# Last steps of the recurrent layer: u split ahead of the scan, another order of loads, two merge tiles ahead of the last gate products

## What is computed

```python
def rglru_block(x, w_in, conv_w, conv_b, w_a, b_a, w_i, b_i, lam, w_out):
    proj = jnp.einsum("bsd,de->bse", x, w_in)
    u, gate = jnp.split(proj, 2, axis=-1)
    u_pad = jnp.pad(u, ((0, 0), (CONV_WIDTH - 1, 0), (0, 0)))
    u = conv_b + sum(u_pad[:, tap:tap + S] * conv_w[tap] for tap in range(CONV_WIDTH))
    ub = u.reshape(B, S, RNN_BLOCKS, RNN_BLOCK_WIDTH)
    r = jax.nn.sigmoid(jnp.einsum("bsnc,ncd->bsnd", ub, w_a).reshape(B, S, RNN_WIDTH) + b_a)
    i = jax.nn.sigmoid(jnp.einsum("bsnc,ncd->bsnd", ub, w_i).reshape(B, S, RNN_WIDTH) + b_i)
    log_a = -LRU_C * r.astype(jnp.float32) * jax.nn.softplus(-lam.astype(jnp.float32))
    a = jnp.exp(log_a)
    bterm = jnp.sqrt(-jnp.expm1(2.0 * log_a)) * (i * u).astype(jnp.float32)
    _, h = lax.associative_scan(combine, (a, bterm), axis=1)   # h[t] = a[t] h[t-1] + bterm[t]
    y = h.astype(x.dtype) * jax.nn.silu(gate)
    return jnp.einsum("bse,ed->bsd", y, w_out)
```

## Time and profile before

| | |
|---|---|
| time, median of 3 runs | 2415.93 us (2414.43 to 2416.19) |
| span of the profiled execution | 2414.6 us |
| PE busy | 2365.7 us, 98% |
| VectorE, ScalarE, GpSimd busy | 1354.1, 1121.3, 617.7 us |
| granted PE clock, 2150 to 2200, 2200 to 2250, 2250 to 2300 us | 1.00, 0.97, 0.97 |
| PE busy in the same three stretches of 50 us | 45.6, 47.5, 46.1 us |

### The profile page before, as it was taken

The page is one execution under the profiler, slowest core; times in us unless marked ns, Lnnn a source line. Parts: engine busy times, 40 slices in busy tenths (PEclk is TensorE's granted clock), DMA queues, the critical chain, the costliest instruction groups (busy, mean ns, idle before and its releaser), DMA issues. The chain is left out here.

```text
span 2414.6 us, 36438 instructions
## 1 busy us (share of the span) xinstructions
PE 2365.7 (98%) x13373; PEld 2031.6 (84%) x13373; DVE 1354.1 (56%) x2772; ACT 1121.3 (46%) x2060; POOL 617.7 (26%) x718
## 2 busy tenths in 40 slices
PE   9999999999999999999999999999999999999998
PEld 7888889998888888888888888878888888887787
DVE  4221211331106888888888888836535565767733
ACT  2111111311116888888888888812014565657300
POOL 0000000000001555545555545516420000000343
PEclk9999999999999999999999999999999999999999
DMA  6443443332234455555445665275533354538762
GB/s 211 139 121 112 116 128 108 118 124 83 84 110 103 110 117 125 136 137 117 112 112 124 137 136 117 78 246 183 187 106 119 119 159 131 148 124 256 243 232 78
DMA packets 221258, 328.77 MB, mean 136 GB/s; under 512 B 17421, under 2 KB 144717, under 8 KB 215261
## 3 DMA queue, kind: packets, MB, share of 16 engines
q1 hardware_dynamic: 220568, 325.91, 47.7%
q0 software_dynamic: 512, 0.53, 0.1%
HBM read 199.89 MB, written 126.48 MB: 135 GB/s over the span
## 5 line engine op out<-in xcount | busy, mean ns | idle before, releaser
L985 DVE TENSOR_TENSOR at_pl<-at_tps,at_ph 128x512 fp32r<-128x512 f32 (+3 forms) x640 | 371.0, 604 | 15.9 <-ACT at_ph L908 15.9
L908 ACT ACTIVATE at_ph<-at_tps 128x512 fp32r<-128x512 f32 (+3 forms) x640 | 318.6, 537 | 125.4 <-PE at_tps L822 117.4
L822 PE MATMUL at_tps<-ident,at_probs 128*128 128x128 f32 x2176 | 340.4, 274 | 8.4 <-DVE at_pl L985 7.1
L380 ACT ACTIVATE pa_stg<-pa_ps 128x512 fp32r<-128x512 f32 (+1 forms) x120 | 71.7, 598 | 575.4 <-PE pa_ps L272 569.5
L842 PE MATMUL at_ops<-at_ph,at_val 128*128 128x256 f32 (+1 forms) x1152 | 315.4, 296 | 0.2 <-DVE at_pl L985 0.2
L898 ACT ACTIVATE at_probs<-at_probs,at_least 128x128 f32<-128x128 f32 (+15 forms) x256 | 308.1, 1204 | 0.0
L272 PE MATMUL pa_ps<-pa_xh,pa_wh 128*128 128x512 f32 x760 | 298.9, 393 | 0.0
L272 PE MATMUL pa_ps<-pa_xh,pa_wl 128*128 128x512 f32 x760 | 297.3, 391 | 0.0
L272 PE MATMUL pa_ps<-pa_xl,pa_wh 128*128 128x512 f32 x760 | 296.9, 391 | 0.0
L842 PE MATMUL at_ops<-at_pl,at_val 128*128 128x256 f32 (+1 forms) x1152 | 295.0, 282 | 0.0
L808 PE MATMUL at_sps<-at_k,at_q 128*128 128x512 f32 (+3 forms) x640 | 277.7, 434 | 9.7 <-DVE at_probs L977 7.2
(11 more groups left out here) (203 smaller groups left out, 4516.0 us busy)
## 6 DMA issues: line engine op xcount, KB each, us to landing
at_q<-q_halves SPq DMA_DIRECT2D x45, 512.0 KB
at_k<-k_halves SPq DMA_DIRECT2D x45, 512.0 KB
q_halves<-pa_stg SPq DMA_DIRECT2D x32, 512.0 KB, 3.8
k_halves<-pa_stg SPq DMA_DIRECT2D x32, 512.0 KB, 3.7
v_halves<-pa_stg SPq DMA_DIRECT2D x32, 512.0 KB, 3.0
y_gated<-re_work SPq DMA_DIRECT2D x32, 512.0 KB, 2.9
at_val<-v_halves SPq DMA_DIRECT2D x15, 1024.0 KB, 17.4
pa_wst<-in_attn_w_in SPq DMA_DIRECT2D x14, 1024.0 KB, 7.2
```

Of the source, the lines that this page charges most:

```text
L380: nc.scalar.activation(out, source(kind, s), func, scale=scale).then_inc(evac_h, 1)
L822: mm = nc.tensor.transpose(tps[c % TB][:, k, :], probs[s % ROWS][:, t0:t0 + P], ident[:, :])
L908: nc.scalar.activation(ph[g % 2][:, j * PB:j * PB + n, i % 2 * P:(i % 2 + 1) * P], tps[c % TB][:, 0:n, :], ACT.Copy).then_inc(high_out, 1)
L985: nc.vector.tensor_tensor(pl[g % 2][at], tps[c % TB][:, 0:n, :], raw(ph[g % 2][at]), ALU.subtract)\
```

## The change

SP: in steps 12 and 13 the output weights are issued ahead of the store of y, and u of step 15 ahead of the store of y of step 12. y for merge tiles 0 and 1 is loaded in four pieces (six of the eight feature blocks for each half, then, after a wait for the y store of step 12, the other two). It was issued ahead of the store of tile 60 and is now issued behind that of tile 61. `load_y(1, 2)` and the gain go ahead of the store of y of step 14, which waits behind `gates` of step 15. PE: merge tile 1 goes ahead of the gate products of step 15. ScalarE: four weight blocks are converted behind tile 59 and four behind the sigmoids of step 13 (before: behind the sigmoids of step 13 and behind tile 61); the square roots of merge tiles 0 and 1 go together behind step 14's root. VectorE: `split_u(14)` goes between `convolve(14)` and `scan(12)`, `split_u(15)` between `convolve(15)` and `scan(13)`; `add_rows` of merge tiles 0 to 3 and the scans of steps 14 and 15 are interleaved anew.

```diff
@@ load_y
                 if r == 1:
-                    sp.wait_ge(y_stored, 32 * (STEPS - NC + j // 2 + 1))
                     if j < 4:
                         sp.wait_ge(products, chunk_done(2 + j // 2))
                     else:
                         sp.wait_ge(m_products, ST + 2 * (j - 4) + 2)
+                    if j == 0:
+                        for l in range(2):
+                            sp.dma_start(raw(m_rows(1, 0)[:, l, 0:KC - CT, :]), m_y[1][:, l, 0:KC - CT, 0:YW])\
+                                .then_inc(y_loaded[0], 16)
+                        sp.wait_ge(y_stored, 32 * (STEPS - NC + 1))
+                        for l in range(2):
+                            sp.dma_start(raw(m_rows(1, 0)[:, l, KC - CT:KC, :]), m_y[1][:, l, KC - CT:KC, 0:YW])\
+                                .then_inc(y_loaded[0], 16)
+                        return
+                    sp.wait_ge(y_stored, 32 * (STEPS - NC + j // 2 + 1))
@@ SyncE, steps 12 to 15 (before, they were in the loop over all steps)
+            for n in range(STEPS - 4, STEPS):
+                first, second = step_tiles(n)[0]
+                if n < STEPS - 2:
+                    load_u(n + 1)
+                store_tile(first)
+                if n < STEPS - 1:
+                    load_gate(n - 1)
+                store_tile(second)
+                if n == STEPS - 2:
+                    load_y(1, 0)
+                    load_y(1, 1)
+                if n == STEPS - 1:
+                    for m in range(RING):
+                        load_residual(1, m)
+                    load_gate(n - 1)
+                    load_y(1, 2)
+                    sp.wait_ge(gates, STEPS)
+                    load_gain(1)
+                if n == STEPS - 4 or n == STEPS - 3:
+                    load_weights(n - STEPS + 4)
+                if n == STEPS - 3:
+                    load_u(n + 2)
+                    sp.wait_ge(y_stored, 32 * (STEPS - NC))
+                store_y(n - 1)
             load_gate(STEPS - 1)
-            for j in range(2, 4):
-                load_y(1, j)
-            sp.wait_ge(gates, STEPS)
-            load_gain(1)
+            load_y(1, 3)
@@ TensorE
                 if n == STEPS - 1:
                     merge_tile(1, 0)
+                    merge_tile(1, 1)
                 gate_products(n)
@@ ScalarE
                 if n == STEPS - 3:
-                    for c in range(CP * 2):
+                    for c in range(CP * 2, KC):
                         weights_high(1, c)
...
-                if n == STEPS - 2:
-                    for c in range(CP * 2, KC):
+                if n == STEPS - 3:
+                    for c in range(CP * 2):
                         weights_high(1, c)
-            deviation(1, 0)
+            for n in range(2):
+                deviation(1, n)
             nonlinear(STEPS - 1)
@@ VectorE
+                convolve(n + 1)
+                if n == STEPS - 3:
+                    split_u(n + 1)
                 if n:
                     scan(n - 1)
...
+            for c in range(CP * 2):
+                weights_low(1, c)
+            feed(STEPS - 3)
+            for c in range(CP * 2, KC):
+                weights_low(1, c)
+            remainder(STEPS - 3)
+            convolve(STEPS - 1)
+            split_u(STEPS - 1)
+            scan(STEPS - 3)
             add_rows(1, 0)
-            norm_rows(1, 0)
+            feed(STEPS - 2)
+            add_rows(1, 1)
+            remainder(STEPS - 2)
+            scan(STEPS - 2)
+            for n in range(2):
+                norm_rows(1, n)
+            add_rows(1, 2)
             feed(STEPS - 1)
             remainder(STEPS - 1)
-            add_rows(1, 1)
+            add_rows(1, 3)
             scan(STEPS - 1)
```

More of the change, by code:

```diff
@@ L1434, in _ @@
             load_strip(3)
-            for n in range(STEPS):
+            for n in range(STEPS - 4):
                 before, behind = step_tiles(n)
-                tiles = (*before, *behind)
                 new_block = (n + 1) % NC == 0
-                if n + 1 < STEPS and not new_block:
+                if not new_block:
                     load_u(n + 1)
-                if n == STEPS - 2:
-                    load_y(1, 0)
-                for k, t in enumerate(tiles):
+                for k, t in enumerate((*before, *behind)):
                     store_tile(t)
                     if k == 0:
-                        if n + 1 < STEPS and new_block:
+                        if new_block:
                             load_u(n + 1)
@@ L1449, in _ @@
                             load_gate(n - 1)
-                        if n + 4 < STRIPS and not new_block:
+                        if not new_block:
                             load_strip(n + 4)
-                        if n + 4 < STRIPS and new_block:
+                        else:
                             if n + 5 < STRIPS:
@@ L1456, in _ @@
                                 load_strip(n + 4)
[L1457 to L1462, removed]
+                    if n and k == 2:
                         store_y(n - 1)
-                        if n == STEPS - 4 or n == STEPS - 3:
-                            load_weights(n - STEPS + 4)
-                if n + 4 < STRIPS and new_block:
+                if new_block:
                     if n + 5 < STRIPS:
@@ L1525, in merge_tile @@
                 j = n // 2
-                pe.wait_ge(y_loaded[j % 4], 16 * (j // 4 + (1 if r or j % 4 >= 2 else 0) + (r * (1 if j % 4 < 2 else 2))))
+                pe.wait_ge(y_loaded[j % 4], 16 * (j // 4 + (1 if r or j % 4 >= 2 else 0) + (r * (1 if j % 4 < 2 else 2))
+                                                  + (3 if r and j % 4 == 0 else 0)))
                 if r == 0:
@@ L1624, in _ @@
                     project_tile(t)
-            for n in range(1, ST):
+            for n in range(2, ST):
                 merge_tile(1, n)
@@ L1931, in _ @@
             convolve(0)
[L1932 to L1935, removed]
+            for n in range(STEPS - 2):
                 split_u(n)
@@ L1942, in _ @@
                         split_gate_weights(BLOCKS - 1)
-                    if n == STEPS - 2:
-                        for c in range(CP * 2):
-                            weights_low(1, c)
                     remainder(n - 1)
-                if n + 1 < STEPS:
-                    convolve(n + 1)
+                convolve(n + 1)
+                if n == STEPS - 3:
+                    split_u(n + 1)
                 if n:
@@ L1952, in _ @@
                     split_gate_weights((n + 1) // NC)
-            add_rows(1, 0)
-            norm_rows(1, 0)
+            for c in range(CP * 2):
[7 more added lines that the diff above has]
+            scan(STEPS - 3)
+            add_rows(1, 0)
+            feed(STEPS - 2)
[5 more added lines that the diff above has]
+            add_rows(1, 2)
             feed(STEPS - 1)
             remainder(STEPS - 1)
-            add_rows(1, 1)
+            add_rows(1, 3)
             scan(STEPS - 1)
-            norm_rows(1, 1)
-            for n in range(2, ST - 1):
+            norm_rows(1, 2)
+            norm_rows(1, 3)
+            for n in range(4, ST - 1):
                 add_rows(1, n)
```

## The result

The changed kernel takes 2420.65 us (median of 8 runs, 2419.11 to 2422.79), the kernel before, measured beside it, 2415.05 (8 runs, 2410.02 to 2416.97). The ratio is 1.0026 with a 95% interval of 1.0017 to 1.0036: the medians differ by 5.6 us, and most of the interval (0.17 to 0.36%) lies over the bound of 0.2% that the prediction named. The profiled execution has a span of 2420.7 us (2414.6 before).

What follows compares the result with a forecast made beforehand. TensorE, busy 98% of the span, was taken as the bound. Late y outweighed the closed waits: the last merge tile ends 4.2 us later, span 2418.8, plus 1.3 gives 2420.1 us, range 2415.1 to 2425.4.

Steps and rivals of the forecast that it cites:

- The wait of step 14: PE ahead of step 14's gate products: still waits about 5.6 us, ended by the sigmoids; moving the split wins nothing.
- Transfers of step 12: SyncE's queue: weights go first, u gains 3.4 us, the y store loses 2.8, step 14's tap stays at 2184.55.
- The two readings of the rule: DMA queue: a store's signal waits for weights issued ahead of it, giving 2420.1 us, or does not, giving 2415.1.
- Transfers of step 13: SyncE's queue: the last of seven transfers lands at 2205.3, when Exp of step 13 starts.
- The rule of 1.5 us for each further transfer: DMA queue: one 512 KB store lands in 3.6 us, each further transfer adds 1.5 us.
- y late: Ahead of merge tile 0: y, issued at 2218.4 behind tile 61, takes 10.0 us, so PE idles 9.6 us.
- Part four: Merge tiles: two ahead of gate products and VectorE's new order remove 5.3 + 1.1 us of waits and 1.65 of clock.
- The sum: End of the last merge tile: 2410.9, 4.2 us later than before; span 2418.8, plus 1.3 gives 2420.1 us.
- T15: Start of ScalarE's tap of step 15, forecast at 2210.25 (2210.38 before).
- (a): Rival, PE's idle time: all waits go, 14.1 us won, 2401.8 us; chance 5%.
- (b): Rival, step 12's transfers: the weights do not hold the stores back, 2415.1 us; chance 13%.
- (c): Rival, load of y: caught in a crowd, 15.0 instead of 10.0 us, 2425.4 us; chance 16%.

Runs made afterwards that it cites:

- experiment 2: The kernel before with only the split of u of step 14 moved ahead of the scan of step 12: 2417.08 us, ratio 1.0009.
- experiment 3: The changed kernel with step 12's transfers reordered to store of y, then u, then weights: 2417.40 us, ratio 1.0014.
- experiment 1: The changed kernel with the load of y for merge tiles 0 and 1 ahead of the store of tile 60: 2410.34 us, ratio 0.9983.
- experiment 4: The kernel before with y for merge tiles 0 and 1 loaded behind the store of tile 61: 2420.43 us, ratio 1.0025.
- experiment 6: The changed kernel with y early and merge tile 1 back behind the gate products on PE: 2410.09 us, ratio 0.9977.
- experiment 7: The changed kernel with y early and VectorE's and ScalarE's old order behind the scan of step 13: 2420.46 us, ratio 1.0023.
- experiment 9: The changed kernel, y early, u before weights in step 12, step 14's split behind the scan, tiles 60 and 61 copied before step 13's Exp: 2404.01 us.
- experiment 5: The changed kernel with y loaded ahead of tile 60's store and step 12 ordered store of y, u, weights: 2407.99 us, ratio 0.9966.

## Why the prediction was right, point by point

- **The wait of step 14** was to stay, at 5.6 us, and to be ended by the sigmoids. It is 7.0 us and names L1694; 1.1 of the 1.4 us more come from the next point. Experiment 2 shows the mechanism alone: the split ahead takes nothing away.
- **Transfers of step 12.** The store was to land at 2179.6, it landed at 2180.7, and the tap of step 14 came at 2185.66, 1.1 us after the forecast. Experiment 3 shows that it is the place in the queue. The two readings of the rule were 2420.1 and 2415.1 us; the store landed in 7.7 us, so it was held back. The Trainium skill ("DMA: Bandwidth & Descriptors", "Queues, rings and completion order") says that a DMA's semaphore increment lands only after every earlier write from that DMA engine. The 7.7 us agree with that, but they would also if the 2 MB of weights were simply moved first, and no run tells the two apart.
- **Transfers of step 13.** Exp was forecast at 2205.3 and came at 2207.41; the error of 1.1 us was handed on and 1.0 added. The rule of 1.5 us for each further transfer is slightly low: from the first weights' issue to the landing it came to 1.8 us in step 12 and 1.6 in step 13.
- **y late.** Issued at 2220.38 (2218.4 forecast), waited for until 2230.92: 10.5 us against 10.0. PE's wait is 9.7 us, against 9.6. Experiments 1 and 4 show it from both sides: 10.3 us less without it, 5 to 6 us more with it in the kernel before. One reading of the prediction is wrong here: the load before did not go out "with steps to spare". Issued at 2200.99 and landed 15.0 us later, it was there at 2216.0, 2.2 us ahead of merge tile 0 (2218.20).
- **Part four** was to close all waits on additions, and did. But the prediction named VectorE's order and the two tiles in front as one thing. By experiments 6 and 7 the first is worth 9 to 10 us where y is early, the second nothing that can be measured.
- **The sum.** The last merge tile ends at 2412.86, 2.0 us after the forecast, all of it from the transfers' terms (T15 2.0 late, y 0.5) less 0.5 of clock (the 29.42 us are 1.8 over 27.46 + 0.2; 2.2 was taken). The median came out 0.5 us from 2420.1 all the same, and that is luck. The prediction added 1.3 us to its span of 2418.8, taking the profiled execution of the kernel before for one 1.3 us under the median; but that compared a span with a time. In every execution on record the time is 1.75 to 1.86 us over the span, so 2414.6 stands for about 2416.4 us, 0.5 over the median. The profiled execution of the changed kernel (2422.5 us) lies 1.9 us over its own. The two errors, 1.9 us too little and 1.3 too much, nearly cancel. The difference, 5.6 us, is larger than the 4.2 forecast and lies on the other side of the 4.8 us at which the chance of "slower" begins: the 52% for "same" against 43% for "slower" leaned a little the wrong way. The step is the one above, two transfers' terms, each 1 us too small, and both too small the same way.

The rivals: (a) is refuted, since two waits stayed, though it had its material: the order with y early, u first and the copies ahead (experiment 9) is 10.9 us faster than the kernel before, of the 14.1 it named. (b) is refuted by the landing in 7.7 us. (c) did not come about: y landed in 10.5 us, which is only 0.1 short of the 10.6 at which the prediction let it count, and in experiment 3 the same four pieces took 9.7.

## What to carry to other kernels

A wait for two things bears the name of the later one; before moving work off it, look up when the other one ends, here 0.07 us sooner. When loads are reordered, write down for each the instruction behind which it now stands in the queue and when that is released: a load issued 17 us before its data were needed, of which it took 15, was put behind a copy that ends when they are needed. And an addition or a store that others wait for belongs between the pieces of a long chain on its engine, not behind them, while a load that the next step needs goes ahead of one that has time.

## What the runs showed of the hardware

- Half-speed stretches do not follow from a wait's length alone. After 2.8 us of wait (experiments 3 and 5) the gate products ran at full clock, and so did merge tile 4 after 3.8 us (experiment 2, 1.00 from 2277.67 to 2282.67); after 2.2 us (experiment 5, with 16.7 us of work in between) about eight matmuls ran at half speed. The wait of 1.95 us ahead of merge tile 3 had such a stretch behind it in the kernel before (0.66 over the first 5 us), and the same wait of 1.96 us in experiment 2 had none (1.00). Granted clocks of experiment 5, gate products and first merge tile:

```profile
2197.76:2203.60 5.84, 5.84 (x25) 4.75 (x26) 5.84 (x6) 3.65 (x4) 0.00 (x0) 1.00 1.07 325
2216.72:2228.00 11.28, 11.28 (x43) 9.17 (x44) 6.32 (x7) 4.58 (x7) 0.00 (x0) 0.85 0.93 304
```

- DMAs that only follow a store in the queue may make it land later. From the issue of step 12's first y store to Exp of step 13 it took 9.4 us in four traces with y's pieces right behind (experiments 1, 5, 6 and 7), 8.8 us in the changed kernel and 7.8 in experiment 3, which have none. I had expected what stands behind in the queue to cost the one ahead nothing. But the last two differ by 0.9 us between themselves, with the same queue in this stretch, so the size is open (0.6 to 1.6 us), and whether it is the pieces' traffic that does it was not tried by itself.
